# Decay levels of a gated linear attention: moving only the right half-blocks of the queries

## What is computed

```python
log_f = jnp.log(lb + (1.0 - lb) * jax.nn.sigmoid(z))
b = jnp.cumsum(log_f)                                  # over time
decay = jnp.exp(jnp.where(causal, b[t] - b[s], -inf))  # for each t, s and key channel k
attn[t, s] = sum_k q[t, k] * k_[s, k] * decay[t, s, k]
o = attn @ v
```

## Time and profile before

| | us |
|---|---|
| median of 3 runs (lowest, highest) | 1040.57 (1040.48, 1042.54) |
| the profiled execution, its own time | 1043.96 |
| its span in the trace | 1042.2 |
| TensorE busy in it | 1030.7 (99%) |
| VectorE busy | 630.7 (61%) |
| ScalarE busy | 473.4 (45%) |
| GpSimd busy | 70.4 (7%) |
| stage of the levels and the values, 612 to 705 us | 93 |

### The profile page before, as it was taken

The page is one execution under the profiler, slowest core; times in us unless marked ns, Lnnn a source line. Parts: engine busy times, 40 slices in busy tenths (PEclk is TensorE's granted clock), DMA queues, the critical chain, the costliest instruction groups (busy, mean ns, idle before and its releaser), DMA issues.

```text
span 1042.2 us, 13517 instructions
## 1 busy us (share of the span) xinstructions
PE 1030.7 (99%) x5010; PEld 852.6 (82%) x5010; DVE 630.7 (61%) x649; ACT 473.4 (45%) x550; POOL 70.4 (7%) x85
## 2 busy tenths in 40 slices
PE   9999999999999999999999999999999999999998
PEld 6888888787877888888888888887888888888887
DVE  6545456654667645455674488885877776455453
ACT  6434445555444634443544452255446344434442
POOL 2000000130100100000010002243000000000000
PEclk9999999999989999999999999999999999999999
DMA  9665647564224465655646553335336556555551
GB/s 310 233 193 189 200 162 227 179 201 139 84 81 162 155 191 179 201 164 198 227 157 198 174 174 103 119 122 162 122 121 202 178 186 201 173 194 192 194 173 41
DMA packets 116664, 178.78 MB, mean 172 GB/s; under 512 B 5640, under 2 KB 73488, under 8 KB 116496
## 3 DMA queue, kind: packets, MB, share of 16 engines
q1 hardware_dynamic: 115808, 174.82, 51.3%
q0 software_dynamic: 512, 1.71, 0.6%
q10 hardware_dynamic: 304, 1.70, 0.6%
HBM read 177.15 MB, written 2.63 MB: 173 GB/s over the span
## 4 chain that ended last, share of the span: by engine, by line
PE 95%; POOL 2%; DVE 2%; issue 1%; ACT 1%; DMA 0%; SPq 0%; ACTq 0%; POOLq 0%
PE gu L519 14%; PE gu L522 14%; PE gu L523 14%; PE acc L519 11%; PE acc L523 11%; PE acc L522 11%; PE tp L519 3%; PE tp L523 3%; PE tp L522 3%; PE acc L889 2%; PE tp L659 1%; POOL rstd L1491 1%; PE gu L766 1%; PE acc L748 1%; PE tp L562 1%; PE acc L778 1%
## 5 line engine op out<-in xcount | busy, mean ns | idle before, releaser
L1570 DVE TENSOR_TENSOR wlo<-raw,whi 128x2048 fp32r<-128x2048 f32 x149 | 345.3, 2321 | 184.6 <-ACT whi L1072 183.8
L1072 ACT ACTIVATE whi<-raw 128x2048 fp32r<-128x2048 f32 x150 | 286.4, 1912 | 144.3 <-PE acc L523 93.0
L519 PE MATMUL gu<-whi,act_hi 128*128 128x512 f32 x592 | 235.1, 397 | 0.0
L522 PE MATMUL gu<-wlo,act_hi 128*128 128x512 f32 x592 | 230.9, 390 | 0.0
L523 PE MATMUL gu<-whi,act_lo 128*128 128x512 f32 x592 | 230.7, 390 | 0.0
L523 PEld LDWEIGHTS gu<-whi,act_lo 128*128 128x128 f32 x592 | 111.2, 188 | 23.9
L519 PEld LDWEIGHTS gu<-whi,act_hi 128*128 128x128 f32 x592 | 111.2, 188 | 22.9 <-DVE act_lo L1596 0.5
L522 PEld LDWEIGHTS gu<-wlo,act_hi 128*128 128x128 f32 x592 | 111.3, 188 | 21.7
L519 PE MATMUL acc<-whi,hT_hi 128*128 128x512 f32 x240 | 93.7, 390 | 0.0
L523 PE MATMUL acc<-whi,hT_lo 128*128 128x512 f32 x240 | 93.4, 389 | 0.0
L522 PE MATMUL acc<-wlo,hT_hi 128*128 128x512 f32 x240 | 93.4, 389 | 0.0
(11 more groups left out here) (276 smaller groups left out, 1351.6 us busy)
## 6 DMA issues: line engine op xcount, KB each, us to landing
raw<-in_w_in SPq DMA_DIRECT2D x96, 512.0 KB, 4.5
raw<-in_down SPq DMA_DIRECT2D x66, 512.0 KB, 4.0
raw<-in_gate SPq DMA_DIRECT2D x64, 512.0 KB, 4.0
raw<-in_up SPq DMA_DIRECT2D x64, 512.0 KB, 4.9
raw<-in_w_out SPq DMA_DIRECT2D x16, 512.0 KB, 4.7
raw<-in_w_branch_hg SPq DMA_DIRECT2D x8, 512.0 KB, 4.3
raw<-in_w_branch_attn SPq DMA_DIRECT2D x8, 512.0 KB, 4.8
post<-in_post_gains SPq DMA_DIRECT2D x3, 512.0 KB, 5.3
```

The lines of the kernel that those rows point to most:

```text
L519: pe.matmul(out, hi, w_hi, start=start, stop=False)
L522: pe.matmul(out, hi, w_lo, start=False, stop=False)
L1072: act.activation(split_weights(k)[0], raw[:, k % RING, :], ACT.Copy).then_inc(hi_ready, 1)
L1570: dve.tensor_tensor(w_lo, raw[:, k % RING, :], w_hi.bitcast(F32), ALU.subtract).then_inc(lo_ready, 1)
```

## The change

For n = 1 to 7 only the right half-blocks of the queries are moved, 64 columns for each head instead of 128, picked with a stride (`right_of`). The stationary operand is the same as before. The outcome is packed, 64 columns for each head, so 8 heads fill one bank, and odd and even levels take different banks. TensorE's level (n, t) now waits for the copy of level n-2 (for n = 1 of n = 0). The predicated copy moves 128 x 512 elements, contiguous in PSUM and strided in SBUF; masks are half as wide. `attnT` is laid out with the head inside, and the last level's copy waits on VectorE's own copy before it. n = 0, `hg_across` and `hg_values` keep their work.

```diff
-    lv = np.zeros((P, len(LEVELS), P), np.float32)
+    lv = np.zeros((P, len(LEVELS), P // 2), np.float32)
     for n, m in enumerate(LEVELS):
-        lv[:, n, :] = (row // (2 * m) == col // (2 * m)) & (row // m % 2 == 0) & (col // m % 2 == 1)
+        right = np.arange(P)[np.arange(P) // m % 2 == 1][None, :]
+        lv[:, n, :] = (row // (2 * m) == right // (2 * m)) & (row // m % 2 == 0)
...
-        level = sb("level", [P, len(LEVELS), P], U8)
+        level = sb("level", [P, len(LEVELS), P // 2], U8)
...
-        with nc.sbuf_tensor("hg_attn", [P, 8, 3, P], F32) as attnT:
+        with nc.sbuf_tensor("hg_attn", [P, 3, 8, P], F32) as attnT:
...
+        def right_of(ap, m):
+
+            return ap.rearrange("p (b two m) -> p b two m", two=2, m=m)[:, :, 1, :]
...
-                    pe.wait_ge(hg_copied, TT * (n - 1) + t + 1)
+                    pe.wait_ge(hg_copied, TT * max(n - 2, 0) + t + 1)
                 for h in range(8):
-                    out = acc[:, t, h // 4, h % 4 * P:(h % 4 + 1) * P]
-                    if n == len(LEVELS):
-                        mm = pe.matmul(out[0:64, 64:P], k_at(t, h)[:, 0:64], q_at(t, h)[:, 64:P], start=True, stop=True)
+                    if n == 0:
+                        mm = pe.matmul(acc[:, t, h // 4, h % 4 * P:(h % 4 + 1) * P], k_at(t, h), q_at(t, h),
+                                       start=True, stop=True)
                     else:
-                        mm = pe.matmul(out, k_at(t, h), q_at(t, h), start=True, stop=True)
+                        m = LEVELS[n - 1]
+                        keys = 64 if m == 64 else P
+                        out = acc[0:keys, t, n % 2, h * 64:(h + 1) * 64].rearrange("p (b m) -> p b m", m=m)
+                        mm = pe.matmul(out, k_at(t, h)[:, 0:keys], right_of(q_at(t, h), m), start=True, stop=True)
...
-            act.activation(attnT[:, :, 1, :], heads(acc[:, 0, :, :].rearrange("p b n -> p (b n)"), 8), ACT.Copy)\
+            act.activation(attnT[:, 1, :, :], heads(acc[:, 0, :, :].rearrange("p b n -> p (b n)"), 8), ACT.Copy)\
...
-            pool.dma_start(post[:, 0:len(LEVELS) * P], level_d).then_inc(tail_in, 16)
+            pool.dma_start(post[:, 0:len(LEVELS) * P // 2], level_d).then_inc(tail_in, 16)
...
-                dve.tensor_copy(level[:, :, :].rearrange("p l n -> p (l n)"), post[:, 0:len(LEVELS) * P])
+                dve.tensor_copy(level[:, :, :].rearrange("p l n -> p (l n)"), post[:, 0:len(LEVELS) * P // 2])
...
-                src = heads(acc[:, t, :, :].rearrange("p b n -> p (b n)"), 8)
-                dst = attnT[:, :, 2 * t, :]
+                src = heads(acc[:, t, :, :].rearrange("p b n -> p (b n)"), 8) if n == 0 else \
+                    heads(acc[:, t, n % 2, :], 8)
+                dst = attnT[:, 2 * t, :, :]
...
-                    ins = dve.tensor_copy(dst[0:64, :, 64:P], src[0:64, :, 64:P])
+                    dve.wait_ge(hg_copied, TT * (n - 1) + t + 1)
+                    ins = dve.tensor_copy(dst[0:64, :, 64:P], src[0:64, :, :])
                 else:
-                    ins = dve.copy_predicated(dst, level[:, n - 1:n, :].to_broadcast([P, 8, P]), src)
+                    m = LEVELS[n - 1]
+                    to = right_of(dst.rearrange("p h n -> p (h n)"), m)
+                    mask = level[:, n - 1:n, :].to_broadcast([P, 8, 64])
+                    ins = dve.copy_predicated(to, mask, src)
```

More of the change, by code:

```diff
@@ L909, in hg_values @@
                     if t:
-                        pe.matmul(o, attnT[:, h, 1, :], v[0], start=True, stop=False)
-                    mm = pe.matmul(o, attnT[:, h, 2 if t else 0, :], v[t], start=not t, stop=True)
+                        pe.matmul(o, attnT[:, 1, h, :], v[0], start=True, stop=False)
+                    mm = pe.matmul(o, attnT[:, 2 if t else 0, h, :], v[t], start=not t, stop=True)
                 mm.then_inc(hg_o, 1)
```

## The result

| | before | after |
|---|---|---|
| median of 5 runs (lowest, highest), us | 1040.57 (1040.48, 1042.54) | 1046.49 (1044.89, 1046.71) |
| ratio | | 1.0041, 95% interval 1.0026 to 1.0055 |
| profiled span, us | 1042.2 | 1044.7 |

A forecast was written before the change was run, and what follows sets the result against it. The prediction took TensorE, busy for 1030.7 of 1042.2 us, to bound the kernel. All terms on its path were 0, so 1043.96 + 0.0 on the profiled execution, 1040.5 us as median, range 1038.5 to 1042.6.

The forecast's parts named there:

- Levels n = 1 to 6 on TensorE: TensorE's 192 level instructions: 0.111 us each before and after, set by the stationary operand's load; 0.0 us.
- The predicated copy: VectorE's 12 copies of 1.322 us fall to about half, 7.7 us less there, none on the path.
- Start: Kernel start: masks' cast falls from 0.620 to some 0.31 us and their transfer halves; TensorE stays busy, 0.
- the sum: Whole kernel: profiled execution 1043.96 us plus 0.0; the same difference carried to the median gives 1040.5 us.
- Rival 1: Levels on TensorE: moving columns are the limit after all, 8.5 us faster, 1032.0 us; chance 0.07.
- rival 2: Levels m = 1 and 2: strided moving operand read slower, at four times 1043.8 to 1047.2 us; chance 0.04.
- Rival 3: TensorE's granted clock falls, 6 us at half pace costing about 3 us, 1043.5 us; chance 0.03.
- The bank wait: TensorE's wait for a free bank before a level: never late, 0.70 us to spare, so loosening gives 0.
- the last copy's wait: Last level's copy waiting for VectorE's own copy before it: already in that order, 0 on the path.
- attnT's layout: attnT: operands stay 128 contiguous columns for each head, ScalarE's one copy becomes contiguous; 0.

The follow-up runs named there:

- e1: Changed kernel plus 448 unused bytes a partition behind the smaller `level`, so later tiles lie where they lay before: 1041.77 us, ratio 0.9992.
- e2: Kernel before the change with only hT_hi and hT_lo moved 64 bytes further on: 1046.43 us, ratio 1.0038.
- e10: Changed kernel, hT back on its old spot, levels n = 1 to 6 moving only 32 of 64 right columns: 1042.03 us, ratio 0.9992.
- e9: Changed kernel, hT back on its old spot, levels n = 1 to 6 using only the first 64 keys: 1036.87 us, ratio 0.9939.
- e7: Kernel before the change with a 128-byte gap ahead of whi, moving whi and all tiles behind it: 1041.97 us, ratio 0.9999.
- e6: Kernel before the change with 128-byte gaps ahead of whi and behind wlo, so tiles behind them move 256: 1059.82 us, ratio 1.0171.

## Why the prediction was wrong

- **The step that failed** is the one that stood without a term: "Levels n = 1 to 6 on TensorE", "The predicated copy" and "Start" price what the smaller masks cost in work, and the sum "1043.96 + 0.0" takes for granted that products which the diff doesn't touch keep their price. The smaller `level` moves every tile behind it by 448 bytes, which costs 4.5 us in hT's 720 products and gives 0.5 us in proj's 192. e1 and e2 show it from both sides. None of the rivals had it: each looked for a gain or a loss in the products of the levels or in the clock.
- **Levels, 192 instructions at 0.111 us before and after, 0.0 us: right.** L897 is as L889 was, and e10 and e9 show the reason given. The Trainium skill's section "LDWEIGHTS (loading the stationary operand)" on the page "TensorE: Matmul & The Clock Gate" makes the load go by the stationary operand's columns; e9 agrees, with 0.067 us for 64 of them against 0.106 for 128, first start to the next product's start.
- **Rival 1** (columns are the limit) and **rival 2** (the stride is read slower): both fall. Each level n = 1 to 6 takes the same 1.70 us, those of m = 1 and 2 included.
- **Rival 3** (the clock): the fall near 297 us is there before and after and unrelated; in the levels the clock stays at 1.00.
- **The bank wait, the last copy's wait, attnT's layout, the start: 0, right** as far as TensorE's waits show; e1 holds them all and is level with the kernel before. The masks' cast took 0.389 us rather than some 0.31, with no effect on TensorE.
- **The predicated copy: the size was off.** I had put 12 x 0.64 = 7.7 us for the twelve, from a row of another operation in which the run length doesn't matter. It matters here. The timeline of DVE after, m = 1 and then m = 4, and the line group:

```profile
634.34 1.35 DVE L2073 COPY_PREDICATED hg_attn<-level,acc 128x512 f32<-128x512 uint8 x1
...
651.76 0.71 DVE L2073 COPY_PREDICATED hg_attn<-level,acc 128x512 f32<-128x512 uint8 x1
```

```profile
L2073 DVE COPY_PREDICATED hg_attn<-level,acc 128x512 f32<-128x512 uint8 x12 | 11.0, 920 | 0.4
```

  The four copies of m = 1 and 2 take 1.31 to 1.35 us, no less than the full 1024 elements before, the eight with runs of 4 or more 0.70 to 0.73. The twelve save 15.9 - 11.0 = 4.9 us on VectorE instead of 7.7, and VectorE is busy for 74.74 us in the stretch, where I had expected about 70. As the prediction said, none of it is on the path.
- **Open:** by what mechanism the distance counts. In the trace the load of the next stationary operand overlaps the matmul before it, so that both operands are read at the same time, but no run here shows whether that is the cause. Nor is it shown what distances other than 0, 32, 64, 128 and 192 cost, or whether products with fewer than 512 moving columns care much.

## What to carry to other kernels

When TensorE is the bound, a change of a tile's size is a change to every product whose operands lie on the two sides of it. Before judging an edit, compare the places of the untouched operands. And try the tiles that TensorE reads together at a multiple of 256 bytes from each other: here one gap of 128 bytes decides between 1042 and 1060 us (e7 and e6). And to know whether fewer moving columns pay, look for a product with the same stationary operand and few columns; with 128 stationary float32 columns, 8, 32 and 64 moving ones were no cheaper than 128 here.

## What the runs showed that I had not expected

- In a long run of them, a product with 512 moving columns takes 227 ns when the starts of the moving and the stationary tile are a multiple of 256 bytes apart, and 230 to 234 ns on average at a distance of 32, 64, 128 or 192. On the 3648 products with weights in whi or wlo that is 17.8 us (e6, 0.0171 x 1041.97).
- In the changed kernel, at distance 64, the pattern of the slow products is regular: 236 and 231 ns by turns.
- A predicated copy with 512 elements whose target has runs of 1 or 2 floats takes 1.31 to 1.35 us, with runs of 4 or more 0.70 to 0.73.
